# Gate, up and up3 projections: one 512-column matmul on a row of rounded x and remainder, with later drains moved

## The reference

```
h = silu(x @ w_gate) * (x @ w_up)              # second layer, 5632 hidden features
x = layer_norm(ALPHA * x + h @ w_down)
...
h = square(relu(x @ w_up))                     # third layer, 8192 hidden features
x = layer_norm_3(ALPHA * x + h @ w_down)
```

## Time and profile before

| | |
|---|---|
| median of 3 runs | 3687.05 us |
| the profiled execution | 3686.9 us |
| its span in the trace | 3684.8 us |
| mean granted TensorE clock | 0.976 |
| TensorE matmul busy | 3476.2 us (94%), 22856 instructions |
| weight loads busy | 3189.9 us (87%) |
| VectorE busy | 2239.9 us (61%) |
| ScalarE busy | 1580.1 us (43%) |
| DMA moved | 608.69 MB, mean 165 GB/s |

### The profile page before, as it was taken

One profiled execution on the slowest core, in us unless ns is written; L12 is line 12 of the kernel. 1 busy time (PEld: TensorE's weight loads), 2 busy tenths in 40 slices (PEclk: granted clock), 3 DMA queues, 4 the chain that ended last, 5 costly groups with the idle time before them and its releaser, 6 DMA issues.

```text
span 3684.8 us, 56355 instructions
## 1 busy us (share of the span) xinstructions
PE 3476.2 (94%) x22856; PEld 3189.9 (87%) x22856; DVE 2239.9 (61%) x2908; ACT 1580.1 (43%) x1876; POOL 6.3 (0%) x9
## 2 busy tenths in 40 slices
PE   8999999999999856789999999989999999999998
PEld 8898998888798846679999988889999799998886
DVE  6667555555659966655444456776766644446766
ACT  4345544344333341233333345543445344445554
POOL 0000000000000000000000000000000000000000
PEclk9999999999999988999999999999999999999999
DMA  6455566666665520055666656654545566655554
GB/s 195 125 163 152 160 195 195 207 200 191 194 178 148 155 71 0 23 177 183 182 182 182 182 170 193 192 156 132 166 144 177 176 203 182 182 182 177 191 195 150
DMA packets 324281, 608.69 MB, mean 165 GB/s; under 512 B 28365, under 2 KB 42703, under 8 KB 322840
## 3 DMA queue, kind: packets, MB, share of 16 engines
q1 hardware_dynamic: 317752, 587.46, 52.9%
q10 hardware_dynamic: 6368, 19.01, 1.3%
HBM read 604.29 MB, written 2.10 MB: 165 GB/s over the span
## 4 chain that ended last, share of the span: by engine, by line
PE 85%; DVE 9%; issue 3%; ACT 2%; DMA 1%; DVEq 0%; SPq 0%; ACTq 0%
PE ps L569 26%; PE ps L570 26%; PE ps L571 26%; DVE arena L1543 2%; DVE w_lo L1537 1%; DVE xtok L1543 1%; DVE arena L1537 1%; ACT w_hi L1126 1%; PE ps L1041 1%; DVE arena L2298 1%; PE ps L1052 1%; PE ps L1049 1%; DMA ring<-in_w_in 1%; PE ps L741 0%; PE ps L872 0%
## 5 line engine op out<-in xcount | busy, mean ns | idle before, releaser
L1537 DVE TENSOR_TENSOR w_lo<-ring,w_hi 128x1024 fp32r<-128x1024 f32 (+2 forms) x1144 | 1371.0, 1202 | 1262.2 <-ACT w_hi L1126 1074.8
L1126 ACT ACTIVATE w_hi<-ring 128x1024 fp32r<-128x1024 f32 (+2 forms) x1144 | 1187.8, 1042 | 1704.9 <-PE ps L569 1636.8
L569 PE MATMUL ps<-x_hi,w_hi 128*128 128x256 f32 x4816 | 1380.1, 287 | 22.4 <-DVE w_lo L1537 21.0
L570 PE MATMUL ps<-x_lo,w_hi 128*128 128x256 f32 x4816 | 1370.6, 285 | 0.0
L571 PE MATMUL ps<-x_hi,w_lo 128*128 128x256 f32 x4816 | 1370.1, 284 | 0.0
L569 PEld LDWEIGHTS ps<-x_hi,w_hi 128*128 128x128 f32 x4816 | 931.4, 193 | 29.6 <-DVE w_lo L1537 20.3
L570 PEld LDWEIGHTS ps<-x_lo,w_hi 128*128 128x128 f32 x4816 | 931.5, 193 | 0.9 <-issue 0.2
L571 PEld LDWEIGHTS ps<-x_hi,w_lo 128*128 128x128 f32 x4816 | 930.8, 193 | 0.3
L569 PE MATMUL ps<-w_hi,h_hi 128*128 128x512 f32 x864 | 337.9, 391 | 9.5 <-DVE h_lo L1537 9.5
L570 PE MATMUL ps<-w_lo,h_hi 128*128 128x512 f32 x864 | 337.6, 391 | 0.0
L571 PE MATMUL ps<-w_hi,h_lo 128*128 128x512 f32 x864 | 337.4, 390 | 0.0
(11 more groups left out here) (330 smaller groups left out, 2598.8 us busy)
## 6 DMA issues: line engine op xcount, KB each, us to landing
ring<-in_w_in SPq DMA_DIRECT2D x416, 512.0 KB, 3.7
ring<-in_w_down SPq DMA_DIRECT2D x216, 512.0 KB, 4.2
ring<-in_w_gate_up SPq DMA_DIRECT2D x176, 512.0 KB, 3.7
ring<-in_w_up SPq DMA_DIRECT2D x128, 512.0 KB, 3.8
ring<-in_w_out SPq DMA_DIRECT2D x64, 512.0 KB, 4.5
ring<-in_w_branch SPq DMA_DIRECT2D x36, 512.0 KB, 4.3
ring<-in_w_in SPq DMA_DIRECT2D x48, 384.0 KB, 3.2
ring<-in_w_o SPq DMA_DIRECT2D x32, 512.0 KB, 4.7
```

Of the source, the lines that this page charges most:

```text
L569: first = pe.matmul(out, left[0], right[0], start=start, stop=False)
L570: pe.matmul(out, left[0], right[1], start=False, stop=False)
L1126: last = act.activation(w_hi[:, s, :, 0:width], ring[:, s, :, 0:width], ACT.Copy)
L1537: return dve.tensor_tensor(o, a, b, op)
```

## The change

It lays x_hi and x_lo in one array so that for each feature block k the 256 rounded columns and the 256 remainders form a row of 512. In gu and up3 a weight block is then used in two matmuls instead of three: w_hi by all 512 columns, w_lo by the 256 rounded ones. A tile now fills four banks, one per e: half 0 of a bank holds w_hi x_hi + w_lo x_hi, half 1 holds w_hi x_lo, and the two halves have to be added. ScalarE copies half 1 to `f_sg` (`cross_half`), VectorE adds half 0 (`whole`), which frees the banks; Silu or Relu then run in place on `f_sg`. `f_sg` moves from the arena to row 0 of `ln_gb`. `prime_hidden` moves from after the section to before the last pair of tiles, on both engines, and that pair is written out behind the loop (`closes`). `load_ln` moves from the opening to the end of the section.

```diff
-def tiles_of(eng, sec, unroll=False, opens=False):
+def tiles_of(eng, sec, unroll=False, opens=False, closes=False):
-    pairs = n // 2
+    pairs = n // 2 - closes
...
+    if closes:
+        yield 2 * pairs, a, pairs
+        yield 2 * pairs + 1, b, pairs
...
-        x_hi = sb("x_hi", [P, KT, S], F32R)
-        x_lo = sb("x_lo", [P, KT, S], F32R)
+        x_both = sb("x_both", [P, KT, 2, S], F32R)
+        x_hi, x_lo = x_both[:, :, 0], x_both[:, :, 1]
...
-        f_sg = area(16384, 2, 4, S)
+        f_sg = ln_gb[:, 0, :].rearrange("p (u a s) -> p u a s", u=2, a=4)
...
+                    if kind == "wide":
+                        for k in range(CH):
+                            for e in range(width // P):
+                                wv = [v[:, s, k, e * P:(e + 1) * P] for v in (w_hi, w_lo)]
+                                first = pe.matmul(ps[:, 4 * u + e, :], wv[0],
+                                                  x_both[:, c * CH + k].rearrange("p h s -> p (h s)"), start=(c == 0 and k == 0), stop=False)
+                                last = pe.matmul(ps[:, 4 * u + e, 0:S], wv[1], x_hi[:, c * CH + k, :], start=False,
+                                                 stop=(c == chunks - 1 and k == CH - 1))
+                                if k == 0 and e == 0:
+                                    first.then_inc(w_used[(g + c - 1) % RING], 1)
+                        if c == chunks - 1:
+                            last.then_inc(tile_done[u], 1)
+                        continue
...
-            project_opening("gu")
+            project_opening("gu", kind="wide")
...
-            project_opening("up3")
+            project_opening("up3", kind="wide")
...
+            def cross_half(u):
+
+                act.activation(f_sg[:, u], ps[:, 4 * u:4 * u + 4, S:2 * S], ACT.Copy).then_inc(cross_out, 1)
+
+            def hidden_gate(name):
 
                 sec = plan[name]
-                for t, u, it in tiles_of(act, sec, opens=True):
-                    splits(sec, u, it, before=opening(t, then))
+                for t, u, it in tiles_of(act, sec, opens=True, closes=True):
+                    if isinstance(t, int) and t == sec.n - 2:
+                        act.wait_ge(tile_free[1], sec.tiles[1] + 2)
+                        prime_hidden("down2")
+                    splits(sec, u, it, before=opening(t))
+                    act.wait_ge(tile_done[u], sec.tiles[u] + it + 1)
                     if u == 0:
-                        act.wait_ge(tile_done[0], sec.tiles[0] + it + 1)
                         act.wait_ge(tile_free[1], sec.tiles[1] + it)
-                        act.activation(f_sg[:, 0].rearrange("p a s -> p (a s)"),
-                                       ps[:, 0:2, :].rearrange("p a s -> p (a s)"), ACT.Silu).then_inc(tile_free[0], 1)
+                    cross_half(u)
+                    if u == 0:
+                        act.wait_ge(tile_free[0], sec.tiles[0] + it + 1)
+                        act.activation(f_sg[:, 0], f_sg[:, 0], ACT.Silu).then_inc(gate_silu, 1)
...
-            hidden_gate("gu", lambda: load_ln(I["ln2_g_2"], I["ln2_b_2"]))
+            hidden_gate("gu")
             act.wait_ge(tile_free[1], plan["gu"].tiles[1] + plan["gu"].n // 2)
-            prime_hidden("down2")
+            load_ln(I["ln2_g_2"], I["ln2_b_2"])
             root_table()
...
-            for t, u, it in tiles_of(act, sec, opens=True):
-                splits(sec, u, it, before=opening(t, lambda: load_ln(I["ln2_g_3"], I["ln2_b_3"])))
+            for t, u, it in tiles_of(act, sec, opens=True, closes=True):
+                if isinstance(t, int) and t == sec.n - 2:
+                    act.wait_ge(hid_ready, 2)
+                    prime_hidden("down3")
+                splits(sec, u, it, before=opening(t))
                 act.wait_ge(tile_done[u], sec.tiles[u] + it + 1)
+                cross_half(u)
                 v = f_sg[:, u].rearrange("p a s -> p (a s)")
-                act.activation(v, ps[:, 2 * u:2 * u + 2, :].rearrange("p a s -> p (a s)"), ACT.Relu)\
-                   .then_inc(tile_free[u], 1)
                 act.wait_ge(tile_free[u], sec.tiles[u] + it + 1)
+                act.activation(v, v, ACT.Relu).then_inc(relu_done, 1)
+                act.wait_ge(relu_done, t + 1)
                 act.activation(hid[:, ds(4 * t, 4), :].rearrange("p a s -> p (a s)"), v, ACT.Square)\
                    .then_inc(hid_ready, 1)
             act.wait_ge(hid_ready, sec.n)
-            prime_hidden("down3")
+            load_ln(I["ln2_g_3"], I["ln2_b_3"])
...
+            def whole(u, count):
+
+                dve.wait_ge(cross_out, count)
+                return tt(f_sg[:, u], ps[:, 4 * u:4 * u + 4, 0:S], f_sg[:, u], ALU.add)
+
             def hidden_up(name):
                 sec = plan[name]
-                for t, u, it in tiles_of(dve, sec, opens=True):
+                for t, u, it in tiles_of(dve, sec, opens=True, closes=True):
+                    if isinstance(t, int) and t == sec.n - 2:
+                        prime_hidden("down2", 0)
                     splits(sec, u, it, before=opening(t))
-                    if u == 1:
-                        dve.wait_ge(tile_done[1], sec.tiles[1] + it + 1)
-                        dve.wait_ge(tile_free[0], sec.tiles[0] + it + 1)
-                        tt(hid[:, ds(4 * it, 4), :].rearrange("p a s -> p (a s)"), f_sg[:, 0].rearrange("p a s -> p (a s)"),
-                           ps[:, 2:4, :].rearrange("p a s -> p (a s)"), ALU.mult).then_inc(tile_free[1], 1)
+                    halves = whole(u, 2 * it + u + 1)
+                    if u == 0:
+                        halves.then_inc(tile_free[0], 1)
+                    else:
+                        halves.then_inc(up_whole, 1)
+                        dve.wait_ge(up_whole, it + 1)
+                        dve.wait_ge(gate_silu, it + 1)
+                        tt(hid[:, ds(4 * it, 4), :], f_sg[:, 0], f_sg[:, 1], ALU.mult).then_inc(tile_free[1], 1)
...
-            for t, u, it in tiles_of(dve, plan["up3"], opens=True):
+            for t, u, it in tiles_of(dve, plan["up3"], opens=True, closes=True):
+                if isinstance(t, int) and t == plan["up3"].n - 2:
+                    prime_hidden("down3", 1)
                 splits(plan["up3"], u, it, before=opening(t))
-            prime_hidden("down3", 1)
+                whole(u, plan["gu"].n + t + 1).then_inc(tile_free[u], 1)
```

More of the change, by code:

```diff
@@ L311, in build @@
         lam_landed, hid_ready = sem("lam_landed"), sem("hid_ready")
+        cross_out, gate_silu, up_whole, relu_done = (sem(k) for k in ("cross_out", "gate_silu", "up_whole", "relu_done"))
         conv_ready, silu_done, wide_order = sem("conv_ready"), sem("silu_done"), sem("wide_order")
@@ L617, in project, with project_opening @@
                     tile(kind, u, sec.chunk(u, 0), sec.more(it), sec.chunks, src, width, side=side)
-            def project_opening(name, normed=True, side=None):
+            def project_opening(name, normed=True, side=None, kind="F"):
                 sec, base = plan[name], n.now(xTp_used)
@@ L625, in project_opening @@
                     pe.wait_ge(tile_free[u], sec.tiles[u] + it)
-                    tile("F", u, sec.chunk(u, 0), sec.more(it), sec.chunks, stationary(x_hi, x_lo), TW,
+                    tile(kind, u, sec.chunk(u, 0), sec.more(it), sec.chunks, stationary(x_hi, x_lo), TW,
                          (normed, base) if first else None, None if first else side)
@@ L1167, in take_x @@
                     act.wait_ge(xTp_ready, n.next(xTp_ready))
-                    act.activation(x_hi[:, 2 * g:2 * g + 2, :].rearrange("p a s -> p (a s)"), ps[:, 4 + g % 4, :], ACT.Copy)\
+                    act.activation(x_hi[:, 2 * g:2 * g + 2, :], ps[:, 4 + g % 4, :].rearrange("p (a s) -> p a s", a=2), ACT.Copy)\
                        .then_inc(xh_ready, 1)
@@ L1414, in _ @@
             ln_roots()
-            def hidden_gate(name, then):
+            def cross_half(u):
+                act.activation(f_sg[:, u], ps[:, 4 * u:4 * u + 4, S:2 * S], ACT.Copy).then_inc(cross_out, 1)
+            def hidden_gate(name):
                 sec = plan[name]
-                for t, u, it in tiles_of(act, sec, opens=True):
-                    splits(sec, u, it, before=opening(t, then))
+                for t, u, it in tiles_of(act, sec, opens=True, closes=True):
[4 more added lines that the diff above has]
+                    act.wait_ge(tile_done[u], sec.tiles[u] + it + 1)
                     if u == 0:
-                        act.wait_ge(tile_done[0], sec.tiles[0] + it + 1)
                         act.wait_ge(tile_free[1], sec.tiles[1] + it)
-                        act.activation(f_sg[:, 0].rearrange("p a s -> p (a s)"),
-                                       ps[:, 0:2, :].rearrange("p a s -> p (a s)"), ACT.Silu).then_inc(tile_free[0], 1)
+                    cross_half(u)
+                    if u == 0:
```

(7 more changed lines are left out.)

## The result

Four executions of the kernel after gave 3660.86, 3656.25, 3657.86 and 3661.04 us, median 3659.36, against 3687.43 us for the kernel before, executed alongside: 0.9922 of it (95% interval 0.9911 to 0.9934). It is faster, by 28.1 us, where I forecast 41.7 (3645.4 us) and a range of 3639 to 3660, whose upper end it keeps by 0.6 us. The profiled execution took 3660.86 us with a span of 3659.1; its counterpart before had 3686.9 and 3684.8.

What follows compares the result with a forecast made beforehand. TensorE's pace per matmul was taken as the bound. Matmuls -32.4, opening losses +0.3, entries -10.1 and early rounding +0.5 gave -41.7 us: 3645.2 from the profiled 3686.9, median forecast 3645.4, range 3639 to 3660.

Steps and rivals of the forecast that it cites:

- The matmuls: In gu and up3, one fixed cost of 0.0133 us saved in each of 2432 blocks: 32.4 us.
- I take 0.3467: Price in us of a gu or up3 block of one 512 and one 256 matmul, down from 0.3600.
- my ends: Bounds on the block price in gu and up3: 0.3600 us if no fixed cost goes, 0.3333 if two go.
- The drains: Added ScalarE and VectorE passes per gu and up3 tile cost nothing; up3's chunk 3 has 1.05 us to spare.
- `prime_hidden` early in up3: Rounding ahead of the last tile pair makes TensorE wait at chunk 3 in up3, once, by 0.5 us.
- The entries: Into down2 and down3: 13.5 us of stalls and half clock go, chunk 3 late by 1.9 and 1.5, net 10.1.
- The moved load: Norm loads at the start of the down sections stay hidden: taken as 0, bound 0 to 0.6 us a section.
- hand-offs late in every tile: Rival: in up3 each hand-off takes 0.45 us longer, chunk 3 is late, 18 us back: 3663 us; chance 0.11.
- The entries give nothing: Rival: at down2 and down3 chunk 3's split with a fallen clock costs as much as the wait did: 3655.5; chance 0.06.
- The fixed cost belongs to the block: Rival: in gu and up3 the fixed cost stays with the block, not the matmul: 3677.5 us; chance 0.06.
- A weight load that shows: Rival: in gu and up3 one unhidden weight load per block, up to 0.105 us, 255 in all: about 3900; chance 0.04.
- The Trainium skill's 2.5 ns: Rival: fixed cost of 2.5 ns per matmul in gu and up3, saving 6.1 us, not 32.1: 3671.4; chance 0.02.

Runs made afterwards that it cites:

- the first profile: Profiled execution of the kernel after in the first measurement, nothing altered: 3660.86 us, with 353.3 ns a block in both gu and up3.
- the repeat: The kernel after once more, unaltered, five executions: median 3651.22 us, 0.9904 of the kernel before; the profiled one took 3651.81 us.
- the run with the entry's work moved on: Kernel after with batches in alternating order, and ScalarE's product wait, norm loads and table put behind the splits of down chunks 3 to 5: 3646.83 us, 0.9892.
- the run of three 256s: Kernel after with its 512-column matmul split into two of 256, layout, banks, drains and early rounding kept: 3677.72 us, 0.9973 of the kernel before.
- the broken series: Kernel after with chunk 0 of every half-0 tile ordered eight 512s then eight 256s, the other 15 chunks of a tile pair alternating: 3657.29 us.
- Four and four: Kernel after with four 512-column matmuls, then four of 256, per block of rows: 3655.67 us.

## Why the prediction was right or wrong

- **What bounds the kernel:** right. TensorE stays busy through both sections, and what they and the entries gave or kept back was its pace or its waits.
- **The range:** it held by luck. The median stands 0.6 us inside it. Its upper end was made for dead entries or late hand-offs, of which neither came, and the cause that did come had no place in it.
- **The matmuls: the step that failed is "I take 0.3467".** The mechanism was right: one fixed cost per block goes, 13.3 ns. The size was wrong in the first profile: half of it, 6.67 ns, came back as the dearer pace of the alternating series, 16.2 us in all, which the sum had at nothing. The block stood inside my ends (0.3333 to 0.3600) and under the 0.355 that I had named as proof against me, but I took its price from single changes of width that I read off rows printed to 0.01 us: 0.23 and 0.12 fit a sum of 346.7 as well as one of 353.3. "Each pays by its own width" doesn't hold: the start times in the trace of before have 233 and 236 ns for the first two 512s behind the change, in place of 226.7, and 114 and 119 for the first two 256s. In the repeat gu had the very 346.7, up3 353.3, and the time was 3651.81 us; with both at 346.7 the first profile's 3660.86 would be 3644.7, 0.5 from the sum's 3645.2. My sum was the time of the luckier pace.
- **The drains:** right. No hand-off late in 38 tiles but the one behind `prime_hidden`; three 256s in the new layout cost nothing.
- **`prime_hidden` early in up3:** right that it is late once, 0.2 us in place of 0.5.
- **The entries:** right, 11.0 us in place of 10.1. Both stalls went, chunk 3 is the next late thing, the clock stays up. The run with `prime_hidden` moved back brought stall and half clock together; the run with the entry's work moved on took the rest of the wait away.
- **The moved load:** right that TensorE loses nothing. ScalarE did wait for a chunk's transfer behind it, and had three chunks of cover; the timeline of ACT in down3, kernel after:

```profile
3306.20 1.06 ACT L1143 ACTIVATE w_hi<-ring 128x1024 fp32r<-128x1024 f32 x1 [2.52 <-DMA ring<-in_w_down]
```

- **The rivals:** hand-offs late in every tile (3663) was near the time and false in cause, as the windows show. "The entries give nothing" is out by their 11 us. "The fixed cost belongs to the block" (3677.5) is out by the run of three 256s, which is that case, at 3677.72. A weight load that shows (3900) is out: a block takes less than three 256s, not more.
- **The Trainium skill's 2.5 ns** ("TensorE: Matmul & The Clock Gate", section "Back-to-back issue gap") would have given 3671.4 us; the section calls its formula that of an isolated matmul, without the weight load that stands ahead of each one here. The rows with one width at a time give 120.0 and 226.67 ns, 13.3 above the columns in both, in the kernel before and in the runs of three 256s and of both matmuls 512 wide. The measurement decides.

## What to carry to other kernels

Fewer, wider matmuls pay where TensorE is the bound, here 13.3 ns per matmul removed, but interleaving two widths can give part of it back, half of it at the dearer pace. Matmuls of one width put together, a chunk at a time, with the order turned round from chunk to chunk, cost 347.9 ns a block each time; strict alternation cost 346.7 or 353.3, so the batches are no gain over its cheaper pace, but they take the luck out. A price per step that is to be multiplied by thousands must come from a long row of the very series, with the start of the first and the last and their count, not from two neighbours. Work that stands between two stages of the bounding engine (here the first operands of the next one) is worth moving ahead of the last tiles, as the idle time costs once itself and once in the clock behind it.

## What was not expected of the hardware

- The alternating series of 512 and 256 columns has two paces, 353.3 and 346.7 ns a block, from the same instructions at the same granted clock of 1.00. A section holds on to one from the end of its opening; the one change inside a section came at a wait of TensorE. What picks the pace is open. In the four traces with this series (the kernel after, its repeat, the late `prime_hidden`, the broken series) up3 began at the dear pace each time, gu twice at either. Four and four has two paces as well, only 0.8 ns apart.
- A change from 256 to 512 columns makes the next five steps dearer by 6, 9, 1, 5 and 4 ns; a change back makes two cheaper by 7 and 1. At the half clock the steps are 427 and 213 ns without such a pattern. A change of width is not needed for it: where the clock comes back in down2 of the kernel before, among 512s alone, the steps are 231, 236, 228, 232, 231, then 227 ns.
- Stalls of 1.57 and 1.20 us between two matmul starts left the granted clock at 1.00; those of 4.55 us and more, before and in the run with `prime_hidden` moved back, were followed by 0.50.
- The DMA queues moved 343 and 369 GB/s in the windows of 5 us at the two entries, with ring chunks and the norm's rows together, where 238 was the most I had read. The Trainium skill ("DMA: Bandwidth & Descriptors", section "Measured (HBM→SBUF, 128 partitions, SWDGE, issued from GpSimd)") gives about 358 GB/s as what each core gets when both cores of an HBM domain stream. This program ran on one core, and the second window lies a little over that.
